# Expert and router weights with 8 (2) consecutive rows per partition, and transposes that take strided columns

## The chip, the cores and the metric

The kernel runs on one core of a Trainium2 chip. The metric is the device time of one execution in microseconds. Three executions were timed: 653.45 us is their median, 651.17 the lowest and 658.9 the highest.

## What is computed

One step of a diffusion backbone of depth 1, in fp32, for 128 context tokens and 512 latent tokens of width D = 1024. Each token gets a modulation from a conditioning vector, an input projection, attention in 8 heads beside a short convolution, an output projection and a layer norm. A mixture of experts follows, and a second layer norm. The change touches the mixture of experts and the layer norm ahead of it. Cut to that, the reference is:

```python
xs = _layer_norm(ALPHA * xs + ga * mix, ln1_g[l], ln1_b[l])
h = xs * (1 + cf) + sf                                   # input of the experts, "h2" in the kernel
g_prob = jax.nn.softmax(t @ wg + bg)                     # t: all 640 rows of h; 4 groups
g_p, g_idx = lax.top_k(g_prob, 1)
e_prob = jax.nn.softmax(the 4 logits of (t @ we + be) in the chosen group)
e_p, e_idx = lax.top_k(e_prob, 2)                        # two of 16 experts per token
hid = jnp.einsum("nd,edf->nef", t, w_exp_in)             # per expert 1024 x 512
a, up = jnp.split(hid, 2, axis=-1)
act = jax.nn.silu(a) * up * gate[:, :, None]
out = jnp.einsum("nef,efd->nd", act, w_exp_out)          # per expert 256 x 1024
```

Every contraction over the 1024 columns of h is a sum, so the kernel may take the columns in any order, if weights and rows are cut alike. The same holds for the 256 inner columns of an expert.

## The kernel before

Five engines run programs of their own, tied by semaphores, in an order written out by hand. SyncE issues the weight loads, GpSimd the gathers, stores and small loads. Matrix products are done in three passes to keep fp32 accuracy: a weight is split into `w_hi` (ScalarE rounds it) and `w_lo` (VectorE subtracts), an activation in the same way, and the helper `three` (lines 1469 to 1471) multiplies hi by hi, hi by lo and lo by hi.

The 1024 columns are contracted in KD = 8 slices of 128 partitions. Before the change, slice k of a weight holds rows 128k to 128k + 127, one on each partition: partition p holds the rows p, 128 + p, 256 + p and so on. Slice k of the activation is therefore columns 128k to 128k + 127 of h, turned so that the columns lie on partitions.

The last third of the span has three stages. First, tile by tile of 128 tokens (5 tiles, order `T_ORDER`), `mix_out` multiplies by `w_out`, VectorE normalizes the rows and writes them into `h2_held[n]` (lines 1259 and 1261, the last tile in two halves of columns), TensorE transposes each tile in eight pieces (`turn_h2`, line 1696) and multiplies them by the router's weights (line 1707). GpSimd stores the tile to DRAM (`h2_rows`, line 568). TensorE also collects the rows of the first expert by matmuls with a one-hot matrix (`gather_first`, line 1719), for which `h2_held[n]` is the loaded operand. In this stage `mix_out` of tile n + 1 runs ahead of `turn_h2` of tile n on TensorE, and the last tile's pieces stand behind the other work.

Then come 16 experts, one after the other. SyncE loads `w_expert_in` in two halves of 1 MB (line 459) and `w_expert_out` in one piece of 1 MB (line 472), each into one of two slots, as soon as VectorE has read the old contents of the slot (its `w_lo` at line 1274, its `act_lo` at line 1279 for `w_expert_out`). ScalarE rounds each half (line 859) and `w_expert_out` (line 866). GpSimd gathers 128 rows of h for the expert after the next from DRAM (line 574) and stores the 128 result rows of an earlier one (line 579). TensorE does `up_half` (two halves of 12 matmuls with 512 moving columns), `turn_rows` (eight transposes of the next expert's rows, line 1774), `turn_act` (two transposes, line 1808) and `down` (12 matmuls). Two lines stand for many: the loaded operand of a matmul is the second name after the arrow in the profile, the moving one the first, so in `PS<-const,uni` the tile in `uni` is loaded ahead and the identity matrix moves.

The third stage gathers each token's two result rows, adds, normalizes and stores them. It has no TensorE work.

Of the kernel before, what the change touches and what calls it, by code (L numbers as in the profile page):

```python
# [5 lines left out]
def build(nc, ins, outs):  # L6
# [64 lines left out]
    with ctx:  # L71
# [33 lines left out]
        sel = const[:, C_SEL:C_SEL + 2]  # L105
        mask3 = const[:, C_MASK:C_MASK + 3 * SPAN].rearrange("p (a k) -> p a k", a=3)

        def strips(v):
            return v.rearrange("p (k t) -> p k t", t=P)

        def dram(name, shape, dt=fp32):
            return nc.dram_tensor(name, shape, dt, kind="Internal").ap()
# [1 line left out]
        def dap(t, offset, pattern):  # L114
# [39 lines left out]
        ln1_g = uni[:, 3 * D:4 * D]  # L154
        ln1_b = uni[:, 4 * D:5 * D]
        ln_t = [uni[:, 6224:6224 + D], uni[:, 9520:9520 + D]]
        h2_held = [strips(v) for v in (uni[:, D:2 * D], gate_a[:, 1, :], uni[:, 2 * D:3 * D], uni[:, 4 * D:5 * D],
                                       uni[:, 5200:5200 + D])]
        h2_T = uni[:, 10544:10544 + D].rearrange("p (k t) -> p k t", k=KD)
        rt = uni[:, 9520:10240]  # L160
# [194 lines left out]
        def raw_slot(b):  # L355
            return raw[:, b, :].rearrange("p (k n) -> p k n", k=KD)
# [33 lines left out]
        def _(sp):  # L390
# [56 lines left out]
            def expert_in(e, h):  # L447
                slot = e % 2
                if h == 0 or e < 2:
                    sp.wait_ge(s_wlo, e + E0 - 1)  # L450
                else:
                    sp.wait_ge(s_wlp, e - 1)
                if e == 1 and h == 0:

                    sp.wait_ge(s_h2, H2)
                    sp.wait_ge(s_h2t, NT)
                    sp.wait_ge(s_h2s[1], 16)
                src = we_in[e].rearrange("(k p) n -> p k n", p=P)
                sp.dma_start(raw_slot(slot)[:, 4 * h:4 * h + 4, :], src[:, 4 * h:4 * h + 4, :]).then_inc(s_raw[slot][h], 16)

            def expert_out(e):
                slot = e % 2
                if e < 2:

                    sp.wait_ge(s_h2, H2)
                    sp.wait_ge(s_h2t, NT)
                    sp.wait_ge(s_h2s[2 * e], 16)
                    if e == 1:
                        sp.wait_ge(s_v, NT)
                else:  # L470
                    sp.wait_ge(s_olo, e - 1)
                sp.dma_start(raw_o[:, slot, :].rearrange("p (k n) -> p k n", k=2),
                             we_out[e].rearrange("(k p) n -> p k n", p=P)).then_inc(s_rawo[slot], 16)

            for e in range(2):
                expert_in(e, 0)
# [31 lines left out]
        def _(pool):  # L508
# [15 lines left out]
            for h in range(HEADS):  # L524
                for a in range(3):
# [3 lines left out]
                           ins["cache_k"][0, 0][:, 0:P, :].rearrange("h t d -> t h d")).then_inc(s_ck, 16)  # L529
            pool.dma_start(ck_nat.rearrange("p a (h d) -> p a h d", h=HEADS)[:, 1],  # L530
                           ins["cache_k"][0, 0][:, P:2 * P, :].rearrange("h t d -> t h d")).then_inc(s_ck, 16)
            pool.dma_start(wr[:, :, 0:NG], ins["w_router_group"][0].rearrange("(k p) n -> p k n", p=P)).then_inc(s_wrl, 16)
            pool.dma_start(wr[:, :, E_AT:NR], ins["w_router_expert"][0].rearrange("(k p) n -> p k n", p=P)).then_inc(s_wrl, 16)
            pool.dma_start(rb[:, 0:NG], dap(ins["b_router_group"], 0, [[0, P], [1, NG]])).then_inc(s_rb, 16)
            pool.dma_start(rb[:, E_AT:NR], dap(ins["b_router_expert"], 0, [[0, P], [1, NE]])).then_inc(s_rb, 16)

# [28 lines left out]
            for n, t in enumerate(T_ORDER):  # L565

                pool.wait_ge(s_h2, n + 1 if n < NT - 1 else H2)
                pool.dma_start(h2_dram[t * P:(t + 1) * P, :].rearrange("p (k c) -> p k c", k=KD), h2_held[n]).then_inc(s_h2s[n], 16)
            pool.wait_ge(s_lc, 1)
            for n in range(NT):  # L570
                pool.wait_ge(s_h2s[n], 16)
# [71 lines left out]
        def _(act):  # L643
# [277 lines left out]
            with act.If(more > 0):  # L921
                act.wait_ge(s_yst[1], 16 * (NE // 2))
                with act.Fori(0, more) as i:

                    e = act.value_load(over_i[0:1, bass.ds(i + 1, 1)], min_val=0, max_val=NE - 1)
                    act.wait_ge(s_wlo, i + (E0 + NE))
                    act.wait_ge(s_wlp, i + NE)
                    act.wait_ge(s_olo, i + NE)
                    act.dma_start(raw_slot(1), we_in[e].rearrange("(k p) n -> p k n", p=P)).then_inc(s_ovw, 16)
                    act.dma_start(raw_o[:, 1, :].rearrange("p (k n) -> p k n", k=2),  # L930
                                  we_out[e].rearrange("(k p) n -> p k n", p=P)).then_inc(s_ovw, 16)
                    act.wait_ge(s_ovw, 32 * i + 32)
                    act.wait_ge(s_hid, i + NE)
                    nc.scalar.activation(w_hi[:, 1, 0:4 * CH], raw[:, 1, 0:4 * CH], ACT.Copy).then_inc(s_whi, 1)
                    nc.scalar.activation(w_hi[:, 1, 4 * CH:8 * CH], raw[:, 1, 4 * CH:8 * CH], ACT.Copy).then_inc(s_whp, 1)
                    act.wait_ge(s_y, i + NE)
                    nc.scalar.activation(wo_hi, raw_o[:, 1, :].rearrange("p (k n) -> p k n", k=2), ACT.Copy).then_inc(s_ohi, 1)
                    gathered_hi(i + NE, 1)
                    half_tanh(i + NE, 1)
                    act_hi_copy(i + NE, 1)  # L940

                    act.wait_ge(s_y, i + (NE + 1))
                    nc.scalar.activation(y_sb[:, 1, :], PS[:, 6:8, :].rearrange("p a n -> p (a n)"), ACT.Copy).then_inc(s_ya, 1)
# [21 lines left out]
        def _(dve):  # L965
# [242 lines left out]
            for n, t in enumerate(T_ORDER):  # L1208
# [45 lines left out]
                m0, sd = mv[:, n % 2, 0:1], rstd[:, n % 2:n % 2 + 1]  # L1254
                hold = h2_held[n]
                for h in range(2 if last else 1):
                    cs = slice(h * CH, (h + 1) * CH) if last else slice(0, D)
                    ks = hold[:, 4 * h:4 * h + 4, :] if last else hold
                    link(V.scalar_tensor_tensor(out=ks, in0=strips(row[:, cs]), scalar=m0, in1=strips(lin_a[:, j, cs]),
                                                op0=ALU.subtract, op1=ALU.mult))  # L1260
                    V.scalar_tensor_tensor(out=ks, in0=ks, scalar=sd, in1=strips(lin_b[j][:, cs]), op0=ALU.mult,
                                           op1=ALU.add).then_inc(s_h2, 1)
                if n < NT - 2:
                    times_gain(n)
                if 1 <= n < NT - 2:
# [198 lines left out]
        def _(pe):  # L1464
# [223 lines left out]
            def turn_h2(n):  # L1688

                if n >= 1:  # L1690
                    pe.wait_ge(s_h2c, 2 * n)
                for h in range(2):
                    if n == NT - 1 or h == 0:
                        pe.wait_ge(s_h2, n + 1 + h)
                    for k in range(4 * h, 4 * h + 4):
                        mm = T.transpose(PS[:, 4 + h, (k % 4) * P:(k % 4 + 1) * P], h2_held[n][:, k, :], ident)
                    if n == NT - 1 or h == 1:
                        mm.then_inc(s_h2t, 1)

# [10 lines left out]
            def gather_first(n):  # L1710
# [5 lines left out]
                    for h in range(2):  # L1716
                        T.matmul(PS[:, 2 + h, :], zeros, ln1_g[:, 0:CH], start=True, stop=False)
                for k in range(KD):
                    mm = T.matmul(PS[:, 2 + k // 4, (k % 4) * P:(k % 4 + 1) * P], h2_held[n][:, k, :], hot_0[:, n, :],  # L1719
                                  start=False, stop=(n == NT - 1 and k % 4 == 3))  # L1720
                if n == NT - 1:
                    mm.then_inc(s_hgt, 1)
# [42 lines left out]
            def turn_rows(c, b, over=False):  # L1765
# [5 lines left out]
                if not isinstance(c, int) or c >= 1:  # L1771
                    pe.wait_ge(s_glo, c)
                for k in range(KD):
                    mm = T.transpose(PS[:, 2 + k // 4, (k % 4) * P:(k % 4 + 1) * P], hg[:, b, k * P:(k + 1) * P], ident)  # L1774
                mm.then_inc(s_hgt, 1)

            def up_half(c, b, h):
# [25 lines left out]
            def turn_act(c, b):  # L1803
# [1 line left out]
                if not isinstance(c, int) or c >= 1:  # L1805
                    pe.wait_ge(s_alo, c)
                for k in range(2):
                    mm = T.transpose(PS[:, 4, k * P:(k + 1) * P], sil[:, 2, k * P:(k + 1) * P], ident)
                mm.then_inc(s_at, 1)


# [85 lines left out]
```

## Time and profile before

| | |
|---|---|
| median of three executions | 653.45 us |
| the profiled execution, its time | 653.2 us |
| the profiled execution, its span (first to last instruction) | 651.4 us |
| TensorE busy with matmuls | 529.2 us, 81% of the span |
| VectorE busy | 384.0 us, 59% |
| ScalarE busy | 266.4 us, 41% |
| bytes moved by transfers | 143.91 MB in 67,821 packets, 221 GB/s on the mean |
| queue 1 (SyncE's loads and stores) | 54,792 packets, 109.46 MB |
| mean granted TensorE clock | 0.925 of full speed |

The profile is of one execution. Busy time of TensorE is modelled from the starts of its pipelined matmuls. "Landing" of a transfer is the time from its issue to its semaphore. A transfer is cut into packets, each one run of consecutive bytes, and 16 DMA engines work on them; their share is the time that packets took over the time of 16 engines.

### The profile page before, as it was taken

To read this page: it belongs to the slowest core of one execution; us is meant where nothing else is said; L and a number is where in the kernel's file an instruction comes from. 1 tells how busy PE (TensorE), PEld (TensorE's weight loads), DVE (VectorE), ACT (ScalarE), POOL (GpSimd) and SP (SyncE) were. 2 spreads that over 40 slices of the span, in tenths; PEclk is the share of its full clock that TensorE was granted. 3 is DMA by queue.
4 is the path that set the end of the run, shared out by engine and by line. 5 is a ranking of instruction groups with operands and counts; after the bars stand their busy time and mean duration, and the time that the engine had idled before them with its cause. 6 is when DMAs were issued, how large, how long until landed. Compare 5 with 4: busy or idle time off the path is not lost.

```text
span 651.4 us, 8064 instructions
## 1 busy us (share of the span) xinstructions
PE 529.2 (81%) x3208; PEld 441.0 (68%) x3208; DVE 384.0 (59%) x603; ACT 266.4 (41%) x366; POOL 112.6 (17%) x125
## 2 busy tenths in 40 slices
PE   3789999999899988668799999769899999973000
PEld 0568888887599986446578888747778887762000
DVE  1326130633020305777659886779998998855697
ACT  1425120203031215567711122376867887850321
POOL 0007300003000001221000000121221223002764
PEclk9998999999799999799999999878999999996555
DMA  8996993557516022657091012599999999982632
GB/s 295 395 326 204 281 359 137 201 179 204 191 40 251 15 104 63 278 154 200 1 330 59 33 57 101 200 342 354 374 366 382 401 401 400 344 283 74 231 118 107
DMA packets 67821, 143.91 MB, mean 221 GB/s; under 512 B 7208, under 2 KB 15971, under 8 KB 67528
## 3 DMA queue, kind: packets, MB, share of 16 engines
q1 hardware_dynamic: 54792, 109.46, 47.1%
q0 software_dynamic: 10256, 32.33, 14.2%
q10 hardware_dynamic: 2736, 1.61, 0.8%
q8 instruction: 26, 0.43, 0.3%
q14 instruction: 11, 0.09, 0.0%
HBM read 124.97 MB, written 21.25 MB: 224 GB/s over the span
## 4 chain that ended last, share of the span: by engine, by line
PE 49%; DVE 19%; DMA 12%; issue 11%; ACT 7%; SPq 1%; POOL 1%; ACTq 0%; POOLq 0%; DVEq 0%
PE PS L1524 7%; PE PS L1469 6%; PE PS L1525 6%; PE PS L1529 6%; PE PS L1471 6%; PE PS L1470 6%; DMA uni<-in_w_expert_out 5%; DVE w_lo L1274 3%; PE PS L1486 3%; DVE act_lo L1279 3%; DMA raw<-in_w_ada 2%; DMA g<-in_x_prompt 2%; PE PS L1719 2%; PE PS L1707 1%; DVE PS L1088 1%
## 5 line engine op out<-in xcount | busy, mean ns | idle before, releaser
L1469 PE MATMUL PS<-w_hi,act_hi 128*128 128x512 f32 x248 | 101.4, 409 | 5.8 <-DVE act_lo L1284 4.3
L1524 PE MATMUL PS<-act_hi,w_hi 128*128 128x320 f32 x320 | 99.3, 318 | 2.6 <-ACT g L713 1.7
L1471 PE MATMUL PS<-w_hi,act_lo 128*128 128x512 f32 x248 | 98.2, 396 | 0.0
L1470 PE MATMUL PS<-w_lo,act_hi 128*128 128x512 f32 x248 | 98.1, 396 | 0.0
L1525 PE MATMUL PS<-act_lo,w_hi 128*128 128x320 f32 x320 | 97.6, 313 | 0.0
L1274 DVE TENSOR_TENSOR w_lo<-raw,w_hi 128x2048 fp32r<-128x2048 f32 x32 | 73.1, 2286 | 2.7 <-ACT w_hi L859 2.5
L1529 PE MATMUL PS<-act_hi,w_lo 128*128 128x320 f32 x320 | 73.6, 311 | 0.0
L1524 PEld LDWEIGHTS PS<-act_hi,w_hi 128*128 128x128 f32 x320 | 61.2, 191 | 9.1 <-issue 4.5
L859 ACT ACTIVATE w_hi<-raw 128x2048 fp32r<-128x2048 f32 x32 | 61.1, 1910 | 10.3 <-DMA raw<-in_w_expert_in 6.3
L1525 PEld LDWEIGHTS PS<-act_lo,w_hi 128*128 128x128 f32 x320 | 61.3, 191 | 0.0
L1469 PEld LDWEIGHTS PS<-w_hi,act_hi 128*128 128x128 f32 x248 | 47.7, 192 | 17.7 <-issue 7.1
L1471 PEld LDWEIGHTS PS<-w_hi,act_lo 128*128 128x128 f32 x248 | 47.4, 191 | 10.3
L1529 PEld LDWEIGHTS PS<-act_hi,w_lo 128*128 128x128 f32 x320 | 54.3, 191 | 0.0
L1470 PEld LDWEIGHTS PS<-w_lo,act_hi 128*128 128x128 f32 x248 | 47.7, 192 | 8.9
L993 DVE TENSOR_TENSOR w_lo<-raw,w_hi 128x2048 fp32r<-128x2048 f32 x16 | 36.1, 2289 | 23.1 <-ACT w_hi L655 23.1
L1279 DVE TENSOR_TENSOR act_lo<-uni,act_hi 128x2048 fp32r<-128x2048 f32 x16 | 36.6, 2291 | 10.4 <-ACT act_hi L866 10.4
L548 POOL DMA_DIRECT2D uni<-bias_windows x24 | 16.1, 682 | 135.0 <-DVE small L1088 134.9
L662 ACT ACTIVATE uni<-PS 128x512 f32<-128x512 f32 x12 | 7.2, 598 | 77.4 <-PE PS L1486 77.4
L1088 DVE CUSTOM_DVE_ANT_1 PS<-PS,uni 128x512 f32<-128x512 f32 x32 | 21.5, 712 | 27.4 <-issue 25.9
L574 POOL DMA_INDIRECT uni<-h_rows,uni x15 | 27.0, 1800 | 60.9 <-PE PS L1774 39.2
L1469 PE MATMUL PS<-act_hi 128*128 128x512 f32 x64 | 27.5, 430 | 11.9 <-DVE act_lo L1300 11.9
L655 ACT ACTIVATE w_hi<-raw 128x2048 fp32r<-128x2048 f32 x16 | 30.0, 1914 | 13.8 <-PE PS L1529 13.2
(248 smaller groups left out, 890.0 us busy)
## 6 DMA issues: line engine op xcount, KB each, us to landing
raw<-in_w_expert_in SPq DMA_DIRECT2D x32, 1024.0 KB, 10.6
raw<-in_w_ada SPq DMA_DIRECT2D x24, 1024.0 KB, 9.1
uni<-in_w_expert_out SPq DMA_DIRECT2D x16, 1024.0 KB, 10.5
raw<-in_w_in SPq DMA_DIRECT2D x12, 1024.0 KB, 9.6
expert_rows<-uni POOLq DMA_DIRECT2D x16, 512.0 KB, 7.0
expert_rows<-g POOLq DMA_DIRECT2D x2, 2560.0 KB, 11.5
g<-in_x_sample SPq DMA_DIRECT2D x2, 2048.0 KB, 14.7
raw<-in_w_out SPq DMA_DIRECT2D x4, 1024.0 KB, 7.4
```

What stands on the lines that cost most here:

```text
L655: nc.scalar.activation(w_hi[:, i % 2, half], raw[:, SLOT["w", i], half], ACT.Copy).then_inc(s_whi, 1)
L859: nc.scalar.activation(w_hi[:, b, half], raw[:, b, half], ACT.Copy).then_inc((s_whi, s_whp)[h], 1)
L993: V.tensor_tensor(w_lo[:, i % 2, half], raw[:, SLOT["w", i], half], w_hi[:, i % 2, half].bitcast(fp32), ALU.subtract).then_inc(s_wlo, 1)
L1088: V.tensor_tensor_reduce(out=s2, in0=s2, in1=rows_b, scale=-1.0, scalar=3.0e38, op0=ALU.add, op1=ALU.min, accum_out=nmax[:, v % 2, 4 * sid ...
L1274: V.tensor_tensor(w_lo[:, b, half], raw[:, b, half], w_hi[:, b, half].bitcast(fp32), ALU.subtract).then_inc((s_wlo, s_wlp)[h], 1)
L1279: V.tensor_tensor(wo_lo, raw_o[:, b, :].rearrange("p (k n) -> p k n", k=2), wo_hi.bitcast(fp32), ALU.subtract).then_inc(s_olo, 1)
L1469: T.matmul(out, lh, rh, start=first, stop=False)
L1470: T.matmul(out, lh, rl, start=False, stop=False)
L1471: return T.matmul(out, ll, rh, start=False, stop=last)
L1524: T.matmul(out, a, h_hi[:, k, sl], start=f, stop=False)
L1525: T.matmul(out, a, h_lo[:, k, sl], start=False, stop=False)
L1529: mm = T.matmul(out, b, h_hi[:, k, sl], start=False, stop=l)
```

## The change

The DRAM side of the weight loads is cut in another way: partition p now holds 8 consecutive rows of `w_expert_in` (rows 8p to 8p + 7), 2 consecutive rows of `w_expert_out`, and 8 consecutive rows of the two router weights. Slice k of a weight is then the rows k, 8 + k, 16 + k and so on. To match, slice k of the activation is the columns k, 8 + k, 16 + k, and so on: the transposes and `gather_first` take every 8th column of a row tile (32 bytes apart), `turn_act` every 2nd (8 bytes apart). The halves of the last `h2_held` tile are no longer its left and right 512 columns, but in each group of 8 columns the first four and the last four. The modulation vectors, `w_in` and `w_out` stay as they were. So does the memory layout of `h2_held` and of the stored rows.

```diff
-        def strips(v):
-            return v.rearrange("p (k t) -> p k t", t=P)
+        def block_half(v, h):
+            return v.rearrange("p (t k) -> p t k", k=KD)[:, :, 4 * h:4 * h + 4]
...
-                src = we_in[e].rearrange("(k p) n -> p k n", p=P)
+                src = we_in[e].rearrange("(p k) n -> p k n", p=P)
                 sp.dma_start(raw_slot(slot)[:, 4 * h:4 * h + 4, :], src[:, 4 * h:4 * h + 4, :]).then_inc(s_raw[slot][h], 16)
...
-                             we_out[e].rearrange("(k p) n -> p k n", p=P)).then_inc(s_rawo[slot], 16)
+                             we_out[e].rearrange("(p k) n -> p k n", p=P)).then_inc(s_rawo[slot], 16)
...
-            pool.dma_start(wr[:, :, 0:NG], ins["w_router_group"][0].rearrange("(k p) n -> p k n", p=P)).then_inc(s_wrl, 16)
-            pool.dma_start(wr[:, :, E_AT:NR], ins["w_router_expert"][0].rearrange("(k p) n -> p k n", p=P)).then_inc(s_wrl, 16)
+            pool.dma_start(wr[:, :, 0:NG], ins["w_router_group"][0].rearrange("(p k) n -> p k n", p=P)).then_inc(s_wrl, 16)
+            pool.dma_start(wr[:, :, E_AT:NR], ins["w_router_expert"][0].rearrange("(p k) n -> p k n", p=P)).then_inc(s_wrl, 16)
...
-                pool.dma_start(h2_dram[t * P:(t + 1) * P, :].rearrange("p (k c) -> p k c", k=KD), h2_held[n]).then_inc(s_h2s[n], 16)
+                pool.dma_start(h2_dram[t * P:(t + 1) * P, :], h2_held[n]).then_inc(s_h2s[n], 16)
...
-                    cs = slice(h * CH, (h + 1) * CH) if last else slice(0, D)
-                    ks = hold[:, 4 * h:4 * h + 4, :] if last else hold
-                    link(V.scalar_tensor_tensor(out=ks, in0=strips(row[:, cs]), scalar=m0, in1=strips(lin_a[:, j, cs]),
-                                                op0=ALU.subtract, op1=ALU.mult))
-                    V.scalar_tensor_tensor(out=ks, in0=ks, scalar=sd, in1=strips(lin_b[j][:, cs]), op0=ALU.mult,
-                                           op1=ALU.add).then_inc(s_h2, 1)
+                    ks, zs, a_, b_ = [block_half(v, h) if last else v for v in (hold, row, lin_a[:, j, :], lin_b[j])]
+                    link(V.scalar_tensor_tensor(out=ks, in0=zs, scalar=m0, in1=a_, op0=ALU.subtract, op1=ALU.mult))
+                    V.scalar_tensor_tensor(out=ks, in0=ks, scalar=sd, in1=b_, op0=ALU.mult, op1=ALU.add).then_inc(s_h2, 1)
...
-                        mm = T.transpose(PS[:, 4 + h, (k % 4) * P:(k % 4 + 1) * P], h2_held[n][:, k, :], ident)
+                        mm = T.transpose(PS[:, 4 + h, (k % 4) * P:(k % 4 + 1) * P], h2_held[n][:, k::KD], ident)
...
-                    mm = T.matmul(PS[:, 2 + k // 4, (k % 4) * P:(k % 4 + 1) * P], h2_held[n][:, k, :], hot_0[:, n, :],
+                    mm = T.matmul(PS[:, 2 + k // 4, (k % 4) * P:(k % 4 + 1) * P], h2_held[n][:, k::KD], hot_0[:, n, :],
                                   start=False, stop=(n == NT - 1 and k % 4 == 3))
...
-                    mm = T.transpose(PS[:, 2 + k // 4, (k % 4) * P:(k % 4 + 1) * P], hg[:, b, k * P:(k + 1) * P], ident)
+                    mm = T.transpose(PS[:, 2 + k // 4, (k % 4) * P:(k % 4 + 1) * P], hg[:, b, k::KD], ident)
...
-                    mm = T.transpose(PS[:, 4, k * P:(k + 1) * P], sil[:, 2, k * P:(k + 1) * P], ident)
+                    mm = T.transpose(PS[:, 4, k * P:(k + 1) * P], sil[:, 2, k::2], ident)
```

The same two weight loads stand once more in the part for experts with over 128 tokens, on ScalarE's queue, and are changed alike.

No instruction moves: on every engine the same operations stand in the same order, and only forms differ. On SyncE's queue, at the first experts, a half load of `w_expert_in` was 128 partitions x 4 rows x 512 elements, and `w_expert_out` 128 x 2 rows x 1024; now the rows of a partition are one piece (a count at the end of a row means as many equal rows):

```order
-L459 DMA raw<-in_w_expert_in 128x4x512 x4
-L472 DMA uni<-in_w_expert_out 128x2x1024
-L459 DMA raw<-in_w_expert_in 128x4x512
-L472 DMA uni<-in_w_expert_out 128x2x1024
...
+L459 DMA raw<-in_w_expert_in 128x2048 x4
+L472 DMA uni<-in_w_expert_out 128x2048
+L459 DMA raw<-in_w_expert_in 128x2048
+L472 DMA uni<-in_w_expert_out 128x2048
```

The places of the loads in the queue are unchanged; only the form of each is another. On VectorE, at the last tile's `h2_held`, the four instructions of the two halves (the line numbers differ by the shorter code):

```order
 L1151 RECIPROCAL small<-small 128x1
-L1259 SCALAR_TENSOR_TENSOR uni<-uni,small,raw 128x512
-L1261 SCALAR_TENSOR_TENSOR uni<-uni,small 128x512
-L1259 SCALAR_TENSOR_TENSOR uni<-uni,small,raw 128x512
-L1261 SCALAR_TENSOR_TENSOR uni<-uni,small 128x512
+L1258 SCALAR_TENSOR_TENSOR uni<-uni,small,raw 128x128x4
+L1259 SCALAR_TENSOR_TENSOR uni<-uni,small 128x128x4
+L1258 SCALAR_TENSOR_TENSOR uni<-uni,small,raw 128x128x4
+L1259 SCALAR_TENSOR_TENSOR uni<-uni,small 128x128x4
```

Here too the order is the same, with 128 pieces of four elements in place of 512 in a row.

## Rows read from the trace of the kernel before

**Rows 1.** the page: busy time by engine, and the chain by engine

```profile
PE 529.2 (81%) x3208; PEld 441.0 (68%) x3208; DVE 384.0 (59%) x603; ACT 266.4 (41%) x366; POOL 112.6 (17%) x125
...
PE 49%; DVE 19%; DMA 12%; issue 11%; ACT 7%; SPq 1%; POOL 1%; ACTq 0%; POOLq 0%; DVEq 0%
```

**Rows 2.** stretches: length, busy us by engine, PEclk, DMA share, GB/s

```profile
345.00:393.00 48.00, 48.00 (x264) 41.35 (x263) 40.83 (x93) 9.54 (x13) 2.20 (x4) 1.00 0.11 45
394.00:398.00 4.00, 4.00 (x33) 3.60 (x32) 3.75 (x11) 2.25 (x3) 0.00 (x0) 1.00 0.00 0
409.90:413.60 3.70, 3.69 (x18) 3.69 (x19) 3.53 (x8) 0.00 (x0) 0.00 (x0) 0.52 0.76 305
440.00:482.00 42.00, 39.29 (x184) 32.21 (x184) 41.22 (x50) 30.97 (x27) 9.23 (x8) 0.96 0.99 357
482.00:502.00 20.00, 19.55 (x107) 16.80 (x107) 17.94 (x15) 14.81 (x15) 3.50 (x5) 1.00 1.02 393
502.00:530.00 28.00, 28.00 (x140) 23.49 (x140) 27.14 (x22) 24.61 (x22) 6.43 (x7) 1.00 1.04 398
530.00:561.00 31.00, 29.95 (x145) 24.13 (x143) 27.05 (x22) 24.97 (x22) 8.50 (x6) 1.00 1.03 394
```

**Rows 3.** SyncE in time: three w_expert_out issues

```profile
502.25 0.37 SPq L472 DMA_DIRECT2D uni<-in_w_expert_out  x1
...
530.11 2.00 SPq L472 DMA_DIRECT2D uni<-in_w_expert_out  x1
...
561.16 10.24 SPq L472 DMA_DIRECT2D uni<-in_w_expert_out  x2
```

**Rows 4.** waits between 528 and 585 us: total, times, longest

```profile
ACT w_hi L859 <- DMA raw<-in_w_expert_in: 6.3, 5, 1.8
...
ACT act_hi L866 <- DMA uni<-in_w_expert_out: 1.3, 3, 0.5
```

**Rows 5.** DMA queues, 482 to 561 us: packets, MB, share

```profile
q1 hardware_dynamic: 10268, 24.29, 80.8%
q0 software_dynamic: 2279, 6.86, 21.9%
```

**Rows 6.** DMA queues from 4 to 12 us, 2 KB runs alone

```profile
DMA packets 1486, 3.02 MB, mean 378 GB/s; under 512 B 48, under 2 KB 48, under 8 KB 1486
...
q1 hardware_dynamic: 1486, 3.02, 102.1%
```

**Rows 7.** DMA queues from 346 to 352 us, 4 KB runs alone

```profile
q0 software_dynamic: 144, 0.52, 21.5%
```

**Rows 8.** DMA queues from 266 to 280 us, mostly 20 KB runs

```profile
q0 software_dynamic: 409, 5.48, 97.9%
```

**Rows 9.** the chain in time: start, us, what

```profile
392.16 0.87 PE PS L1696 x8
...
394.75 3.57 PE PS L1719 x32
398.32 1.70 PE PS L1707 x16
...
409.91 3.73 PE PS L1719 x16
...
421.35 4.70 DMA uni<-h_rows,uni
...
488.27 2.13 PE PS L1816 x20
```

**Rows 10.** all engines in time: one gather, the next transposes

```profile
510.90 1.51 POOL L574 DMA_INDIRECT uni<-h_rows,uni  x1 [2.63 <-PE PS L1774]
...
518.39 1.04 PE L1774 MATMUL PS<-const,uni 128*128 128x128 f32 x8
...
527.68 1.04 PE L1774 MATMUL PS<-const,uni 128*128 128x128 f32 x8
```

**Rows 11.** DMA issues: count, median us to landing

```profile
uni<-h_rows,uni POOLq DMA_INDIRECT x15, 8.0
```

More of the change, by code:

```diff
@@ L156, in build @@
         ln_t = [uni[:, 6224:6224 + D], uni[:, 9520:9520 + D]]
-        h2_held = [strips(v) for v in (uni[:, D:2 * D], gate_a[:, 1, :], uni[:, 2 * D:3 * D], uni[:, 4 * D:5 * D],
+        h2_held = [v for v in (uni[:, D:2 * D], gate_a[:, 1, :], uni[:, 2 * D:3 * D], uni[:, 4 * D:5 * D],
                                        uni[:, 5200:5200 + D])]
@@ L928, in _ @@
                     act.wait_ge(s_olo, i + NE)
-                    act.dma_start(raw_slot(1), we_in[e].rearrange("(k p) n -> p k n", p=P)).then_inc(s_ovw, 16)
+                    act.dma_start(raw_slot(1), we_in[e].rearrange("(p k) n -> p k n", p=P)).then_inc(s_ovw, 16)
                     act.dma_start(raw_o[:, 1, :].rearrange("p (k n) -> p k n", k=2),
-                                  we_out[e].rearrange("(k p) n -> p k n", p=P)).then_inc(s_ovw, 16)
+                                  we_out[e].rearrange("(p k) n -> p k n", p=P)).then_inc(s_ovw, 16)
                     act.wait_ge(s_ovw, 32 * i + 32)
```

## Prediction

> **What bounds the kernel now.** I read the page first, for the engines' shares and the chain by engine [rows 1]. TensorE is busy 81% of the span and carries 49% of the chain; VectorE carries 19%, transfers 12%. An average over stages does not say what a stage waits for, so the table of stretches comes next [rows 2]. In 345 to 393 us (output projection and normalization of the tiles) TensorE is busy 48.00 of 48 us, with 45 GB/s on the DMA engines. From 440 to 561 us (the experts) three resources are nearly full: the DMA share is 0.99 to 1.04 at 357 to 398 GB/s, VectorE is busy 41.22 of 42 us up to 482, TensorE 28.00 of 28 us from 502 to 530.
>
> Which of the three sets the pace is read from the issues of the `w_expert_out` load, one per expert [rows 3]. There are seven from 502.25 to 561.16. The first three steps take (530.11 - 502.25) / 3 = 9.29 us each, with TensorE always busy; the last three (561.16 - 530.11) / 3 = 10.35 us. Behind 530 us ScalarE waits 6.3 us for `raw` and 1.3 us for `w_expert_out` to land [rows 4], and TensorE has gaps (29.95 of 31). So the weight loads are behind only at the end: what they cost beyond TensorE's pace is 31.05 - 3 x 9.29 = 3.2 us, plus what the last waits do behind 561.
>
> **The change, part by part.**
>
> *Router weights.* Two loads of 80 KB together on GpSimd's queue, needed 300 us after they are issued. Their pieces in SBUF stay short whatever the DRAM order is. Cost and gain 0; their cover is that whole time.
>
> *Expert weights.* Each half load of `w_expert_in` (1 MB) was 512 runs of 2 KB and becomes 128 runs of 8 KB; each `w_expert_out` was 256 runs of 4 KB and becomes 128 of 8 KB. The trace has no 8 KB load, so I price a byte from stretches with one size of run. Mostly 2 KB: 102.1% of 16 engines for 8 us is 130.7 us of engine time for 3.02 MB, or 43.3 ns per kB (a 2 KB run takes 89 ns) [rows 6]. 4 KB stores: 21.5% of 6 us x 16 is 20.6 us for 0.52 MB, 39.7 ns per kB (a run takes 161 ns) [rows 7]. Mostly 20 KB stores: 97.9% of 14 us x 16 is 219.3 us for 5.48 MB, 40.0 ns per kB [rows 8]. One end for 8 KB is no saving at all over 2 KB (43.3), since [rows 7, 8] are stores and this is a load. The other is the straight line through the first two runs: 161 - 89 = 72 ns for each further 2 KB gives 305 ns for 8 KB, 37.2 ns per kB. I take 39.7, the nearest size in bytes. An expert has 2.10 MB of `w_expert_in`: 3.6 ns x 2,097 kB / 16 engines = 0.47 us. `w_expert_out` is at 39.7 already: 0 here, and 2.5 ns x 1,049 kB / 16 = 0.16 us by the line. So 0.5 us per expert, between 0 and 1.0.
>
> What is that worth? From 482 to 561 us the two queues hold 80.8% + 21.9% of the DMA engines [rows 5]: they never rest. There are about eight experts in it, so 8 x 0.5 = 4 us less work. The stretch takes 79 us, and at TensorE's pace it would take 8 x 9.29 + 2.13 (the twenty overflow matmuls [rows 9]) = 76.4. That is 2.6 us of excess by this count and 3.2 by the last three steps; 4 us of saved transfer covers either. Before 482 VectorE is full [rows 2], so a faster load waits for a free slot and gains nothing. Behind 561 one more wait on `raw` goes, some 0.3 us. What is late next is TensorE, at 9.29 us per expert, with VectorE just under it: the gain is capped there. Gain 3.2 + 0.3 = 3.5 us; bounds 0 and 4.5 (the stall and all of the waits of [rows 4] that lie behind 561).
>
> *Strided columns as TensorE's loaded operand.* This is the part the trace cannot price directly: in every transpose the strided tile is the operand that is loaded ahead of the matmul, and no load of before takes columns 32 bytes apart. The count: `turn_h2` 5 x 8 = 40, `gather_first` 5 tiles x 16 = 80 (each fp32 matmul is two passes), `turn_rows` 15 x 8 = 120; `turn_act` has 2 per expert at 8 bytes. How fast does a load run today? Eight transposes take 0.87 us, 109 ns each; 32 passes with 128 moving columns 3.57 us, 112 ns; 16 passes with only 24 moving columns 1.70 us, 106 ns [rows 9]. The time does not depend on the moving columns, so the load sets it: 106 ns for 128 columns. At the lower level of the clock, 1.2 GHz (0.52 granted in 409.90 to 413.60 against 1.00 [rows 2]), the same 16 passes take 3.73 us, 233 ns each [rows 9]. So at full clock, 2.4 GHz, a load takes two array cycles per column, where a moving column takes one. The loaded operand is thus read at half the rate of the moving one and has time in hand. One end is 0; the other is a load that takes twice as long, +106 ns, whose nearest row is that of the half clock. I take 0, for the two cycles: that is my choice and the least certain step here.
>
> The Trainium skill, page "SBUF — State Buffer", section "Door 1: The DMA port swizzle", speaks against the change: SBUF has 16-byte lines, two hits on a line are needed for full bandwidth, and each access that goes to a new line pays. With fp32 columns 32 bytes apart every column is a new line. By that rule the time would be that of rival B; no row here shows it.
>
> *VectorE on the last tile.* Four instructions take 128 x 4 pieces in place of 512 in a row; the same 512 elements each, and both halves still wait for the whole tile's mean. A row with such pieces is missing. If each took half again of its some 0.7 us (1,280 ns for 1,024 elements elsewhere), that is 1.3 us at most; I take 0. The `h2_rows` store moves the same bytes from the same addresses in the same 4 KB runs (144 packets for 128 rows [rows 7]): 0.
>
> *Sum.* The profiled execution took 653.2 us (span 651.4): 653.2 - 3.5 + 0 + 0 = 649.7 us. It stood 0.25 us under the median of 653.45, so the same sum from the median is 650.0.
>
> **The rivals.**
>
> *B: the strided load takes twice as long* (slower). Every load gets +106 ns. `turn_h2`: 40 x 0.106 = 4.2 us, in stretches with TensorE always busy. `gather_first`: 80 x 0.106 = 8.5 us; TensorE is busy 4.00 of 4 us there [rows 2]. Experts: 8 x 0.106 = 0.85 us, so the pace goes from 9.29 to 10.14 us; from 482 to 561 that is 8 x 10.14 + 2.13 = 83.2 against 79, +4.2 us, and the loads' gain is gone since transfers are no longer late. Before 482 VectorE hides it at 10.5 us per expert. Two experts behind 561 and the first, which the chain passes through right behind its gather [rows 9], add 3 x 0.85 = 2.6. In all 4.2 + 8.5 + 4.2 + 2.6 = 19.5: 672.9 us. It decides against the change from 3.5 / 19.5 of it on, about +20 ns per load. For it: no row excludes it, and the loads are all exposed. Against: the two cycles per column.
>
> *C: the longer runs bring nothing.* The engine time per byte stays at 43.3, because [rows 7, 8] are stores, or the stall behind 530 has another source. Then 653.2. For it: from 4 to 20 KB the price per byte does not fall. Against: 2 to 4 KB differ by 8%.
>
> *D: the loads crowd out GpSimd's gathers.* If an engine takes turns between queues packet by packet, an 8 KB packet (some 310 ns) ahead of each of the eight rows that an engine fetches, in place of 89 ns, adds up to 8 x 0.22 = 1.8 us. A gather is issued at 510.90 and lands 8.0 us later [rows 11], at 518.9; the transposes that use it are the second ones from there, at 527.68 [rows 10], 8.8 us of slack. Only the first gather is on the chain, 4.70 us at 421.35 [rows 9]: up to +1.8 once, 651.5 us.
>
> *E: a part of B*, +20 to +60 ns per load: 653 to 661 us.
>
> **How the numbers follow.** My forecast 0.50 (D in it, as a correction); B 0.25; C 0.13; E 0.08; a gain beyond the cap, by something not seen, 0.04. The time is the forecast's, 650.0; its own range is 648 to 653. The whole range: 0.25 lies at B, around 668 to 675, so the range must reach into it to leave out no more than 2 in 10: 647 to 672. Out of it are half of B and the 0.04 below. What a measurement of this kernel can tell is about 1%, 6.5 us. Slower by more than that: B and most of E, 0.30. Faster by more than that asks for twice what the stall holds: 0.07. The rest, 0.63, is within 1%.
>
> **What would show it.** In the page of the changed kernel: packets of queue 1 down by about 16 x (1,024 + 256 - 384) = 14,300, from 54,792 to about 40,500; if not, the runs were not joined. Issues of `w_expert_out` behind 530 us at 9.3 us each and ScalarE's waits for `raw` near nothing: the gain is as said; still 10.3 us each: C. Eight transposes in 0.87 us and 32 passes of `gather_first` in 3.57 us: no price for the stride; 1.7 and 7 us: B. Time lost before 440 us with equal transposes would make the whole argument wrong, since there I expect no difference over 1 us.

## The result, and the profile after

The changed kernel takes 661.0 us (median; 660.39 to 663.61), against 652.73 us of the kernel before on the same occasion. The ratio is 1.0133, with a 95% interval of 1.0095 to 1.0172: slower by 8 us, and clear of no change. The profiled execution took 661.17 us, its span is 659.4 us, 8.0 us over the span before. The page of the changed kernel, its span, the busy time of the engines, queue 1 (packets, MB, share of 16 engines) and the chain by engine:

```profile
span 659.4 us, 8064 instructions
...
PE 541.2 (82%) x3208; PEld 455.1 (69%) x3208; DVE 384.6 (58%) x603; ACT 267.1 (41%) x366; POOL 107.8 (16%) x125
...
q1 hardware_dynamic: 40456, 109.46, 45.7%
...
PE 60%; DVE 15%; issue 10%; DMA 7%; ACT 5%; SPq 1%; POOL 1%; ACTq 0%; POOLq 0%; DVEq 0%
```

Against [rows 1], TensorE has 12 us more busy time and 60% of the chain, where it had 49%. The transfers went as they were meant to: queue 1 has 40,456 packets, 14,336 fewer, for the same 109.46 MB. Its share times the span is 0.457 x 659.4 = 301.3 us of all 16 engines, where it was 0.471 x 651.4 = 306.8; 5.5 us less over 16 experts, 0.34 us each. (The shares are rounded to 0.1%, so each product is good to 0.3 us.)

The chain in order of time (start, us, what) at the end of the normalization stage:

```profile
392.31 0.88 PE PS L1693 x8
...
394.91 7.48 PE PS L1716 x32
402.39 1.75 PE PS L1704 x16
...
404.98 3.98 PE PS L1716 x16
408.97 1.71 PE PS L1693 x8
...
417.01 4.14 PE PS L1716 x16
...
421.51 3.93 PE PS L1716 x16
```

The rows answer to [rows 9]. Line 1716 is `gather_first`, 1693 `turn_h2` and 1704 the router here. The eight transposes of `turn_h2` take 0.88 us as before (0.87). The 32 passes of `gather_first` take 7.48 us where they took 3.57: 234 ns each in place of 112. The next sixteen take 3.98 us, then 4.14 and 3.93, where the chain before had 1.88, 3.73 and 1.89. The 16 router passes, whose operand is not strided, stay at 1.75 (1.70). The granted clock of these stretches, and two stretches of the experts (length, busy us by engine, PEclk, DMA share, GB/s):

```profile
394.90:402.30 7.40, 7.40 (x35) 7.40 (x33) 4.16 (x9) 1.97 (x2) 0.53 (x1) 1.00 0.18 71
...
405.00:408.90 3.90, 3.90 (x17) 3.90 (x18) 1.73 (x11) 0.00 (x0) 0.00 (x0) 0.50 0.00 0
408.97:410.60 1.63, 1.63 (x9) 1.31 (x8) 0.00 (x0) 0.60 (x1) 0.00 (x0) 0.50 0.00 0
...
417.00:421.00 4.00, 3.99 (x17) 3.99 (x18) 3.76 (x8) 0.00 (x0) 0.00 (x0) 0.50 0.52 219
421.50:425.40 3.90, 3.90 (x20) 3.90 (x19) 0.00 (x0) 0.00 (x0) 0.00 (x0) 1.00 0.77 269
...
502.00:530.00 28.00, 28.00 (x139) 23.65 (x139) 25.43 (x20) 24.52 (x21) 5.60 (x6) 1.00 0.99 393
530.00:561.00 31.00, 31.00 (x153) 26.12 (x152) 29.91 (x25) 27.47 (x24) 7.67 (x7) 1.00 1.01 420
```

Two things are to be seen. First, at full clock (394.90 and 421.50) a strided pass takes 234 to 246 ns; at the lower level (405.00 and 417.00, granted 0.50) 249 and 259 ns, hardly more. With neighbouring columns it was 112 ns at the one level and 233 at the other. These are lengths divided by 16 or 32, and the first pass of a group is longer. Behind it the starts are as far apart at both levels, as TensorE in time shows (third and fourteenth start of the group at the lower level, then the same at full clock):

```profile
417.65 0.44 PE L1716 MATMUL PS<-uni 128*128 128x128 f32 x1
420.28 0.44 PE L1716 MATMUL PS<-uni 128*128 128x128 f32 x1
421.91 0.40 PE L1716 MATMUL PS<-uni 128*128 128x128 f32 x1
424.54 0.40 PE L1716 MATMUL PS<-uni 128*128 128x128 f32 x1
```

That is (420.28 - 417.65) / 11 = 239 ns and (424.54 - 421.91) / 11 = 239 ns: the strided pass does not follow TensorE's clock. A pass with neighbouring columns does: 112 ns at full clock, and (412.85 - 410.72) / 10 = 213 ns at the lower level in the kernel before. So the sixteen passes that ran at the lower level in both kernels lose only 4.14 - 3.73 = 0.4 us. The four groups together lose 3.91 + 2.10 + 0.41 + 2.04 = 8.46 us.

Second, the clock had fallen by 404 (0.97 granted from 402.40 to 404.00, 0.50 from 405.00), where the kernel before still had 1.00 from 405.40 to 406.60. So the eight transposes at 408.97 took 1.71 us in place of 0.87, in a stretch granted 0.50.

The issues of the `w_expert_out` load, one per expert, tell where the time stands later:

```profile
432.58 0.33 SPq L472 DMA_DIRECT2D uni<-in_w_expert_out  x1
...
449.48 0.33 SPq L472 DMA_DIRECT2D uni<-in_w_expert_out  x1
...
512.69 0.33 SPq L472 DMA_DIRECT2D uni<-in_w_expert_out  x1
...
540.72 0.33 SPq L472 DMA_DIRECT2D uni<-in_w_expert_out  x1
...
568.71 9.68 SPq L472 DMA_DIRECT2D uni<-in_w_expert_out  x2
```

They stood at 423.04, 440.02, 502.25, 530.11 and 561.16 before; the last three are [rows 3]. The lag is 9.5 us at 432.58 and 449.48, so most of the loss is there ahead of the second expert. It is still 9.5 us at 481.61 (472.14 before), 10.4 us at 512.69 and 7.6 at 568.71: six steps that took 58.9 us take 56.0. The three steps of 10.35 us behind 530 are gone, each is 9.33 us, and TensorE is busy 31.00 of 31 us from 530 to 561, at 420 GB/s. ScalarE's waits for weights [rows 4] are gone.

The account: 9.5 us lost by the end of `gather_first`, 1.0 lost from 482 to 512, 2.9 won back behind, 0.4 the rest: 8.0 us.

### The profile page after: what moved, and what is told of

The parts are those of the page before. It is cut to its first block, busy times and chain, and to the rows that moved or that the text cites. A ratio compares the mean times of both kernels' runs of the same rounds, so it can differ in the third digit from the quotient of the medians.

```text
span 659.4 us, 8064 instructions
## 1 busy us (share of the span) xinstructions
PE 541.2 (82%) x3208; PEld 455.1 (69%) x3208; DVE 384.6 (58%) x603; ACT 267.1 (41%) x366; POOL 107.8 (16%) x125
## 3 DMA queue, kind: packets, MB, share of 16 engines
q1 hardware_dynamic: 40456, 109.46, 45.7%
## 4 chain that ended last, share of the span: by engine, by line
PE 60%; DVE 15%; issue 10%; DMA 7%; ACT 5%; SPq 1%; POOL 1%; ACTq 0%; POOLq 0%; DVEq 0%
PE PS L1466 9%; PE PS L1468 8%; PE PS L1467 8%; PE PS L1521 7%; PE PS L1522 6%; PE PS L1526 6%; DVE w_lo L1271 3%; PE PS L1716 3%; PE PS L1483 3%; DMA raw<-in_w_ada 2%; DMA g<-in_x_prompt 2%; PE PS L1771 2%; PE PS L1704 1%; DVE g L1430 1%; DVE PS L1088 1%
## 5 line engine op out<-in xcount | busy, mean ns | idle before, releaser
L1618 PE MATMUL PS<-const,uni 128*128 128x128 f32 x136 | 19.8, 289 | 19.5 <-ACT uni L783 11.9
```

## The experiments

My theory after this reading (L): the whole loss is the strided load of the fp32 matmuls of `gather_first`; the transposes pay next to nothing, and the long runs win about 3 us. Rivals: the transposes share the loss (T), or the long runs and the other order of rows in DRAM cause it (M). The first three kernels and the version that keeps the gain ran side by side with the kernel before, whose median there is 654.02 us; the others beside it at 653.92 us.

**Only `gather_first` strided, from the kernel before.**

```diff
-                    mm = T.matmul(..., h2_held[n][:, k, :], hot_0[:, n, :],
+                    mm = T.matmul(..., h2_held[n].rearrange("p k t -> p (k t)")[:, k::KD], hot_0[:, n, :],
```

> The kernel before, with only gather_first changed: it takes every 8th column as its loaded operand, all else (weight loads, transposes) as before. Its result for the first expert's rows is not the reference's; the work is the same. Theory L (the strided load of the fp32 matmuls is the whole loss): 80 passes at 234 ns in place of 112 ns, about +9.5 us over before, 662 us. Rival T (the transposes and what hangs on them share the loss): under +5 us. Rival M (the new order of rows in DRAM or the contention of 8 KB runs is the loss): about 0.

Measured: 663.33 us, ratio 1.0138 (1.0102 to 1.0173). One subscript gives a loss as large as the whole change's. Its chain (start, us, what):

```profile
392.34 0.87 PE PS L1696 x8
...
394.93 7.49 PE PS L1719 x32
...
421.00 4.01 PE PS L1719 x16
```

The same 7.49 us for 32 passes, with every weight load as before. The loss of L is there; T and M are not needed for the 9 us.

**The change, with only `gather_first` put back.**

```diff
-                    mm = T.matmul(..., h2_held[n][:, k::KD], hot_0[:, n, :],
+                    mm = T.matmul(..., h2_held[n][:, k * P:(k + 1) * P], hot_0[:, n, :],
```

> The changed kernel, with only gather_first put back to 128 neighbouring columns; weight loads in long runs and strided transposes stay. The first expert's rows are then not the reference's. Theory L: the loss is gone and the loads' gain is left: about 3 us under before, 650 us, and 32 passes in 3.57 us. Rival T: still at or over before, 653 to 658. Rival M: 661, as the changed kernel.

Measured: 651.59 us, ratio 0.9971 (0.9947 to 0.9995). The chain of this kernel:

```profile
394.70 3.57 PE PS L1716 x32
```

The passes are back at 112 ns and the loss is gone; what is left is a gain of 0.3%.

**Only the expert weights in long runs, from the kernel before.**

```diff
-                src = we_in[e].rearrange("(k p) n -> p k n", p=P)
+                src = we_in[e].rearrange("(p k) n -> p k n", p=P)
...
-                             we_out[e].rearrange("(k p) n -> p k n", p=P)).then_inc(s_rawo[slot], 16)
+                             we_out[e].rearrange("(p k) n -> p k n", p=P)).then_inc(s_rawo[slot], 16)
```

> The kernel before, with only the expert weights loaded in 8 KB runs; columns of the activations as before, so the experts' results are not the reference's. Theory L: the stall behind 530 us goes, -3 us against before, 650 us; steps of w_expert_out at 9.3 us to the end. Rival M: no gain or a loss against before. Theory L and rival T agree here; the difference between this run and e2 is the price of the strided transposes: under 1 us by L, over 3 us by T.

Measured: 651.18 us, ratio 0.9956 (0.9934 to 0.9978), 2.8 us under before. Stretches of its experts (length, busy us by engine, PEclk, DMA share, GB/s):

```profile
502.00:530.00 28.00, 28.00 (x141) 23.54 (x140) 27.15 (x22) 24.55 (x22) 6.14 (x6) 1.00 1.01 407
530.00:561.00 31.00, 31.00 (x155) 26.05 (x154) 30.16 (x24) 27.19 (x23) 6.30 (x6) 1.00 1.01 416
```

TensorE is busy all of both stretches, where it had a gap behind 530 before [rows 2]. The stall was the gain, and TensorE's pace is the cap. Rival M falls. The difference to the run before is 0.4 us by the medians, with overlapping intervals. The steps tell more: with strided transposes (the run before, first two rows) six experts take 56.01 us, with neighbouring columns (this run, last two rows) 55.72. Both are without a stall, so the strided transposes cost 0.05 us per expert.

```profile
502.37 0.33 SPq L472 DMA_DIRECT2D uni<-in_w_expert_out  x1
...
558.38 9.67 SPq L472 DMA_DIRECT2D uni<-in_w_expert_out  x2
```

```profile
503.93 0.33 SPq L472 DMA_DIRECT2D uni<-in_w_expert_out  x1
...
559.65 9.62 SPq L472 DMA_DIRECT2D uni<-in_w_expert_out  x2
```

**All transposes strided.** From the changed kernel, with the loads of the expert weights and `gather_first` put back; the router weights and the 128 x 4 pieces stay as in the change:

```diff
-                src = we_in[e].rearrange("(p k) n -> p k n", p=P)
+                src = we_in[e].rearrange("(k p) n -> p k n", p=P)
...
-                             we_out[e].rearrange("(p k) n -> p k n", p=P)).then_inc(s_rawo[slot], 16)
+                             we_out[e].rearrange("(k p) n -> p k n", p=P)).then_inc(s_rawo[slot], 16)
...
-                    mm = T.matmul(..., h2_held[n][:, k::KD], hot_0[:, n, :],
+                    mm = T.matmul(..., h2_held[n][:, k * P:(k + 1) * P], hot_0[:, n, :],
```

> The kernel before with strided columns in all transposes (turn_h2, turn_rows, turn_act) and the halves of the last tile as in the change; weight loads and gather_first as before. Experts' results are not the reference's. Theory H: 8 transposes in 0.89 us in place of 0.87, +0.05 us per expert, under 1 us in all: 654 to 655 beside 654 of before. Rival T: over 3 us more.

Measured: 654.2 us against 653.92 of before beside it, ratio 1.001 (0.9982 to 1.0038). No difference that can be measured; 192 strided transposes (160 of them 32 bytes apart) cost less than 2.5 us by the interval. Rival T falls.

**What a stride costs in a load.** The changed kernel, with other distances in the first two tiles of `gather_first`:

```diff
+            def step(n, k):
+                return [[1, 1, 2, 2, 3, 3, 4, 4], [5, 5, 6, 6, 7, 7, 8, 8]][n][k] if n < 2 else 1
...
-                    mm = T.matmul(..., h2_held[n][:, k::KD], hot_0[:, n, :],
+                    mm = T.matmul(..., h2_held[n][:, 0:P * step(n, k):step(n, k)], hot_0[:, n, :],
```

> The changed kernel, with gather_first taking, in its first two tiles, columns 1, 1, 2, 2, 3, 3, 4, 4 and 5, 5, 6, 6, 7, 7, 8, 8 elements apart for its eight slices (two passes each), and neighbouring columns in the other three tiles; the first expert's rows are not the reference's. Each pass's start is read from the trace. Theory 16 (a column costs more where it opens a new 16-byte line, and two on a line are free): about 112 ns per pass at 1 and 2, in between at 3, about 234 ns from 4 on, flat to 8. Rival 8 (8-byte unit): 112 at 1, 234 from 3 on, with 2 already dearer. Rival G (the price grows with the distance): rising from 2 to 8, with 234 only at 8.

One execution was profiled (656.47 us); only the starts of its passes are used. Each distance has four passes (two slices, two passes each). The rows are TensorE in time, each from the first pass of a distance on, and the last pass at the end (start, length of the matmuls shown, count):

```profile
396.11 0.50 PE L1719 MATMUL PS<-uni 128*128 128x128 f32 x3
396.55 0.52 PE L1719 MATMUL PS<-uni 128*128 128x128 f32 x3
397.02 0.51 PE L1719 MATMUL PS<-uni 128*128 128x128 f32 x2
397.72 0.63 PE L1719 MATMUL PS<-uni 128*128 128x128 f32 x2
398.65 0.61 PE L1719 MATMUL PS<-uni,raw 128*128 128x128 f32 x2
399.55 0.61 PE L1719 MATMUL PS<-uni,raw 128*128 128x128 f32 x2
400.45 0.62 PE L1719 MATMUL PS<-uni,raw 128*128 128x128 f32 x2
401.37 0.40 PE L1719 MATMUL PS<-uni,raw 128*128 128x128 f32 x1
402.08 0.40 PE L1719 MATMUL PS<-uni,raw 128*128 128x128 f32 x1
```

The steps between the starts, by four: distance 1 takes (396.55 - 396.11) / 4 = 110 ns per pass, 2 takes 118, 3 takes 175, 4 takes 232, 5 takes 225, 6 takes 225, 7 takes 230, and 8 takes (402.08 - 401.37) / 3 = 237. That is theory 16: two fp32 columns in 16 bytes are nearly free, with distance 3 three columns in four open a new piece of 16 bytes, and from 16 bytes on the price is flat. Rivals 8 and G fall: distance 3 is half way and not at 234, and 5 to 8 cost no more than 4. As an estimate from these figures, a pass takes 232 / 128 = 1.8 ns for each piece of 16 bytes that it opens: 116 ns for the 64 pieces of distance 2 (118 measured), 174 for the 96 of distance 3 (175), while distance 1 with its 32 pieces is held at 110 by something else. The same rule stands in the Trainium skill, page "SBUF — State Buffer", section "Door 1: The DMA port swizzle": 16-byte lines, of which each must be hit twice for full bandwidth. The trace agrees: 118 ns at two hits, 232 at one. The same place of the Trainium skill calls a stride of up to 4 fp32 free; as a distance of columns that is not so here, 175 ns at 3 and 232 at 4. For the columns of `turn_act`, 8 bytes apart, the table would give next to no price; they were not measured by themselves.

**Why the transposes don't pay.** The changed kernel, with slices 0 to 3 of `turn_rows` cut to 32 partitions, so that a load still takes 128 columns but only 32 columns move; odd experts take neighbouring columns:

```diff
-                    mm = T.transpose(PS[:, 2 + k // 4, (k % 4) * P:(k % 4 + 1) * P], hg[:, b, k::KD], ident)
+                    rows_in = hg[:, b, k * P:(k + 1) * P] if b else hg[:, b, k::KD]
+                    wide = 32 if k < 4 and not over else P
+                    at = (k % 4) * P
+                    mm = T.transpose(PS[:, 2 + k // 4, at:at + wide], rows_in[0:wide], ident[0:wide, 0:wide])
```

> The changed kernel, with turn_rows cut: slices 0 to 3 transpose 32 partitions only (the load still takes 128 columns, only 32 columns of the identity move), slices 4 to 7 as before; odd experts take neighbouring columns, even ones every 8th. Results are not the reference's. Theory H (a transpose's strided load doubles too, from about 53 to 107 ns, and hides behind the 109 ns of its 128 moving columns): narrow slices at 60 to 70 ns with neighbouring columns, 107 to 120 ns with strided ones; wide slices 109 to 112 ns in both. Rival N (a transpose's load has no price for the stride): narrow slices alike in both kinds of expert.

One execution was profiled (661.02 us). TensorE in time, at a granted clock of 1.00: four narrow transposes and four wide ones of an odd expert (neighbouring columns), then four narrow ones of an even one (strided). The second number runs to the end of the last of the four:

```profile
436.06 0.43 PE L1774 MATMUL PS<-const,uni 32*128 32x32 f32 x4
...
436.42 0.66 PE L1774 MATMUL PS<-const,uni 128*128 128x128 f32 x4
...
444.27 0.62 PE L1774 MATMUL PS<-const,uni 32*128 32x32 f32 x4
```

A single narrow transpose lasts 0.22 us with neighbouring columns and 0.27 strided, by the views of one instruction. So the starts are (0.43 - 0.22) / 3 = 70 ns apart with neighbouring columns and (0.62 - 0.27) / 3 = 117 ns apart strided; wide ones with neighbouring columns (0.66 - 0.27) / 3 = 130, and 109 when a whole group of eight is counted [rows 9]. The first step of each group is the longest: from the second start to the fourth (436.14 to 436.27, 444.40 to 444.62) they are 65 and 110 ns apart. The stride costs a transpose's load too, nearly the double. But 128 moving columns take 109 ns, which hides the whole load with neighbouring columns and all but a few ns of the strided one: eight full transposes take 0.89 to 0.90 us in the changed kernel's chain and 0.87 before. Theory H holds, N falls. That the partition count was cut as well as the moving columns is a limit of this test: the exact time of the load in the full transpose is not shown. By these figures there is no room left; a load dearer than this, or fewer moving columns, would be paid for.

**A version that keeps the gain.** The first expert's `w_expert_in` and the router weights keep the old cut, so that `gather_first` and `turn_h2` take neighbouring columns; all other experts have long runs:

```diff
-                src = we_in[e].rearrange("(p k) n -> p k n", p=P)
+                src = we_in[e].rearrange("(k p) n -> p k n" if e == 0 else "(p k) n -> p k n", p=P)
...
-                        mm = T.transpose(..., h2_held[n][:, k::KD], ident)
+                        mm = T.transpose(..., h2_held[n][:, k * P:(k + 1) * P], ident)
...
-                    mm = T.matmul(..., h2_held[n][:, k::KD], hot_0[:, n, :],
+                    mm = T.matmul(..., h2_held[n][:, k * P:(k + 1) * P], hot_0[:, n, :],
```

> A version that keeps the loads' gain without the strided fp32 load: the first expert's w_expert_in and the router weights keep the old cut (row 128k + p), so gather_first and turn_h2 take neighbouring columns; experts 1 to 15 and all w_expert_out have long runs, and turn_rows and turn_act strided columns. Complete computation. Theory L: -3 us against before, 650 us. Rival T: 652 to 655. Rival M: over before.

Measured: 652.09 us, ratio 0.9959 (0.9937 to 0.998) to the kernel before. It beats both kernels: by 0.4% and, since the change is at 1.0133, by some 1.7%. Its `w_expert_out` issues, in a profiled execution of 647.89 us, the fastest of its twelve:

```profile
499.62 0.33 SPq L472 DMA_DIRECT2D uni<-in_w_expert_out  x1
...
527.64 0.33 SPq L472 DMA_DIRECT2D uni<-in_w_expert_out  x1
...
555.63 9.68 SPq L472 DMA_DIRECT2D uni<-in_w_expert_out  x2
```

Six steps in 56.01 us, 9.33 each, to the end.

**The stride moved to VectorE.** All weights in long runs; VectorE writes `h2_held` already in the new order, reading `row` and the modulation vectors 8 elements apart:

```diff
+        def kept(v, h):
+            w = v.rearrange("p (k t) -> p k t", k=KD)
+            return w if h is None else w[:, 4 * h:4 * h + 4, :]
...
-                    ks, zs, a_, b_ = [block_half(v, h) if last else v for v in (hold, row, lin_a[:, j, :], lin_b[j])]
+                    ks, zs, a_, b_ = kept(hold, g_), block_half(row, g_), block_half(lin_a[:, j, :], g_), block_half(lin_b[j], g_)
```

(`block_half` gives the view with k outermost here.)

> A version with all weights in long runs and no stride on TensorE but turn_act's 8 bytes: VectorE writes h2_held with its columns already in the new order (slice k in 128 neighbouring elements), reading row and the two modulation vectors with a step of 8 elements; the stored and gathered rows carry that order. Complete computation. If VectorE reads a step of 32 bytes at its usual rate (1,285 ns for 1,024 elements): as e4, 651 to 652 us. If it reads at half rate, ten instructions take +1.3 us each; those of the last tile (+2.6 us) are on the chain and some of the rest: 655 to 660.

Measured: 654.68 us beside 653.92 of before, ratio 0.9999 (0.9974 to 1.0025). VectorE's first instruction, of a whole tile and of a half of the last (busy us, mean ns of one), in this kernel:

```profile
L1264 DVE SCALAR_TENSOR_TENSOR uni<-uni,small,raw 128x1024 f32<-128x1024 f32 x3 | 6.7, 2227 | 0.1
...
L1264 DVE SCALAR_TENSOR_TENSOR uni<-uni,small,raw 128x512 f32<-128x512 f32 x2 | 2.3, 1151 | 0.0
```

and in the changed kernel, the second with the 128 x 4 pieces:

```profile
L1258 DVE SCALAR_TENSOR_TENSOR uni<-uni,small,raw 128x1024 f32<-128x1024 f32 x3 | 3.9, 1284 | 0.1
...
L1258 DVE SCALAR_TENSOR_TENSOR uni<-uni,small,raw 128x512 f32<-128x512 f32 x2 | 1.5, 750 | 0.0
```

The kernel before took its 512 elements in a row in the same time:

```profile
L1259 DVE SCALAR_TENSOR_TENSOR uni<-uni,small,raw 128x512 f32<-128x512 f32 x2 | 1.5, 749 | 0.0
```

A step of 32 bytes makes VectorE 1.73 times as slow (2,227 ns for 1,284), and the second instruction, with the step in one tensor of two, as slow (2,213 ns), while pieces of 16 bytes, 32 apart, cost nothing. The loads' 3 us are about used up by it. That the two cancel is read from the medians; the permuted write with the old loads was not run. The profiled executions fit it: the `w_expert_out` issue that stood at 423.04 in the kernel before came 4.3 us later (427.31), the last one 2.0 us later (563.12 for 561.16).

## Why the prediction was wrong, step by step

The forecast was 650.0 us, with 647 to 672 for the range; 661.0 lies in the range, but the sign is wrong: a gain was forecast and a slowdown came, where I had put 0.63 on no change and 0.30 on a slowdown. It is neither the forecast nor B as priced (672.9); it lies in the range only since the range had to reach to B, which is luck. My own signs came out split: eight transposes in 0.88 us (no price), 32 passes in 7.48 us (B). And 9.5 us were lost before 440 us with equal transposes, which I had said would make the whole argument wrong.

- *What bounds each stage*: right. The stall behind 530 us was the loads', and TensorE's pace was next.
- *Price of a byte in 8 KB runs*: right in kind, a little high. I took 0.5 us per expert; the queue's engine time fell by 0.34.
- *Gain 3.5 us*: right. The six steps won 2.9 us, the loads alone 2.8 us (ratio 0.9956). Rival C falls. So does D: the first gather took 4.67 us where it had taken 4.70.
- *Router weights, the 128 x 4 pieces, the stored rows*: nothing speaks against 0. The pieces took 750 ns for 512 elements, as the row of 512 before (749). The kernel with all transposes strided has the first two and the same time as before; none of the three was changed alone.
- *Strided columns, the step that failed*: I took 0 "for the two cycles", holding that an operand read at half the moving rate "has time in hand". In `gather_first` it has none: from 16 bytes on an fp32 pass takes 234 ns in place of 112, 8.46 us over the 80 passes. The premise was wrong for these matmuls already in the trace of the kernel before. Its chain has, just ahead of `gather_first` and at a granted clock of 1.00, four fp32 passes with 512 moving columns:

```profile
393.03 1.72 PE PS L1717 x4
```

  That is 430 ns each, 0.84 ns or two array cycles for a moving column, the same as for a loaded one. And the conclusion went from the array's clock to a limit that does not follow it: 239 ns per strided pass at full clock and at the lower level. The rule that I had cited against the change (the Trainium skill, page "SBUF — State Buffer", section "Door 1: The DMA port swizzle") was right for `gather_first`, and I had given B, the time that I derived from it, a quarter of the chance.
- *B's own sum failed too*, in its terms. `gather_first` was put at 8.5 us and its passes lost 8.46. That they agree so well is in part luck: 64 passes paid 122 to 131 ns, more than the 106 that I took, and the sixteen that ran at the lower clock in both kernels paid 26. From the start of `gather_first` to its end the chain gained 9.4 us, with the transposes at the lowered clock among it. But `turn_h2` (4.2) and `turn_rows` (4.2 + 2.6) came to 0.01 us per tile at full clock and 0.05 us per expert. I had read "the load sets it" from fp32 passes with 24 and 128 moving columns and carried it over to transposes, of which I had only the 128-column form. There the moving columns set the 109 ns, and the load has room for about as much as the stride costs.
- *Rival E* (+20 to +60 ns per load, 653 to 661 us) gave the time but not the mechanism: no load pays an amount between, the passes of `gather_first` pay all and the transposes 3 ns or so each.

Open: the 1.0 us lost from 482 to 512. It comes with the strided `gather_first` and not with the loads or the transposes. The three steps from the issue at 481.61 to that at 512.69 take 31.08 us in the changed kernel and 30.11 before. With only `gather_first` strided it is 30.98, with only `gather_first` put back 30.21. The two slower ones were granted 0.91 of the clock from 482 to 502, the two faster ones 1.00. Why the clock fell there is not shown. Open too: why an fp32 matmul's pass takes 110 ns and a narrow transpose 65, with the same 128 columns to load (strided 234 and 110).

## What to carry to other kernels

Price a strided operand by the unit that reads it and by what that unit waits for: a load that hides behind 128 moving columns can nearly double for next to nothing, the load of a matmul that is itself load-bound doubles the matmul. Check a premise on the rate of an operand against a row with the same type. Keep two fp32 elements within 16 bytes where a reader is the bound, and put the stride where cover is. When a layout change has one expensive reader, give that reader's data the old layout, here one expert of sixteen, and keep the gain for the rest.

## What the runs showed of the hardware

- A load of 128 fp32 columns by TensorE, as time per pass of an fp32 matmul at full clock: 110 ns at a distance of 4 bytes, 118 at 8, 175 at 12, and 225 to 237 at 16 to 32. At the lower level of the clock (1.2 GHz, granted 0.50) 213 ns with neighbouring columns; strided by 32 bytes it is 239 ns at either level, so the stride's price is nearly gone at the lower one.
- A moving column of an fp32 pass takes 0.84 ns at full clock (512 columns in 430 ns).
- Transposes of 128 columns take 109 to 112 ns either way at full clock; with 32 partitions and 32 moving columns 65 ns with neighbouring columns and 110 strided.
- VectorE takes 1,284 ns for 1,024 fp32 elements in a row and 2,227 with a step of 32 bytes in two inputs, 2,213 in one; pieces of four elements 32 bytes apart run at full rate.
- 14,336 fewer packets for the same bytes took 5.5 us off queue 1's time on 16 engines, 88 us of engine time, or 6 ns for each packet that was saved.
